# Three products of a weight block, to one PSUM bank in a row or to two banks in turn

## The chip, the cores and the metric

The kernel runs on one core of one Trainium2 chip. The time is the device time of one launch in microseconds (us), as the median of several runs. TensorE (PE in the profile) multiplies, with its weight loads in a row of their own (PEld); VectorE (DVE) and ScalarE (ACT) do the elementwise work, and DMAs bring the weights in.

## The reference, cut to what matters

Two transformer-like blocks are applied to one sequence of 512 tokens with 1024 features: a gated linear attention with a convolution branch, pooling, cross-attention to a memory of 256 tokens, two gated feed-forward layers, then a second linear attention, a sliding-window attention and two squared-ReLU layers. Nearly all the arithmetic is products with weight matrices in float32:

```python
h = x @ w_in                                                    # projections, 1024 rows of weights
y = (jax.nn.silu(x @ w_gate) * (x @ w_up)) @ w_down             # ffn, width 2816, twice
u = jax.nn.relu(h @ w_up); y = (u * u) @ w_down                 # mlp, width 4096, twice
```

## The kernel before, in words

**The product.** A float32 product is made from three products of a faster format: each weight tile and each activation tile is split into a high part and a rest (`w_hi`, `w_lo`; `xh`, `xl`), and `mm3` (L629) adds high times high, high times rest and rest times high into one PSUM bank: weights `a[0]` with moving `b[0]`, `a[0]` with `b[1]`, `a[1]` with `b[0]`.

**The units.** Weights come as 207 units of 128x2048 elements (L46), one after the other through two buffers. For each unit SP loads `w_raw`, ScalarE makes `w_hi` (`split_hi`, L1138), VectorE makes `w_lo` (`split_lo`, L1626), and TensorE uses it. ScalarE may overwrite `w_hi` once TensorE has counted the unit as used (`unit_used`).

**Where the change acts.** `feature_unit` (L648) and the first half of a feed-forward chunk, `up` (L890), take a unit as eight blocks (k) of two column halves (m). Half m is summed over k in its own bank. Before, each k issues the three products of m = 0 and then the three of m = 1, so the banks change after every third product. The last product of half 0 raises that bank's `bank_full`, the last product of half 1 raises `unit_used`, which also tells that its bank is full (`full`, L635). `down` (L906), `token_unit` (L663), the stages pool and glr, and all products that aren't of weights keep `mm3` or single products as they are.

**What sets the order.** Each engine runs one program in a fixed order and waits on semaphores. The banks are dealt out ahead (`plan_banks`, L120): successive units of a projection alternate between banks 0, 1 and 2, 3; in the two mlp stages every `up` uses banks 0 and 1, and `down` goes through banks 4 to 7 twice. A unit's readers wait for bank 0's or 2's fullness first and the other's after it: `drain_pair` (ScalarE, L1145), `residual` and `add` (VectorE, L1657, L1675), `mh<-bank,rstd` (L1766), the queries of the window attention (L2221). TensorE waits with `wait_free` for both banks of a unit before its first product.

**The loops.** A feed-forward stage starts with the `up` of chunk 0 ("first"). Then a loop does the `up` of the next chunk ahead of the `down` of the one before. Between stages stand the normalisations: TensorE sums over features with a matrix of ones, ScalarE and VectorE work out mean and root, and VectorE and ScalarE rewrite the activations before TensorE may go on.

Of the kernel before, what the change touches and what calls it, by code (L numbers as in the profile page):

```python
# [29 lines left out]
D, T, P = 1024, 512, 128  # L30
KT = D // P
# [269 lines left out]
def at(i, per, c):  # L301

    return c if i is None else i * per + c
# [71 lines left out]
def build(nc, x, mem, params, consts, table, w_gk2, sinks, w, out):  # L375
    scratch = nc.dram_tensor("rel_scratch", [16, 384], F32, kind="Internal").ap()
    with ExitStack() as ctx:
# [135 lines left out]
        def bank(key):  # L513
            return banks[FILL[key][0]]

        def wait_full(eng, key, i=None):

            b, _, _, unit, n, per = FILL[key]
            if unit is None:
                eng.wait_ge(bank_full[b], at(i, per, n))  # L520
            else:
                eng.wait_ge(unit_used, at(i, per, unit + 1))

        def wait_free(eng, key, i=None):

            b, n, per = FILL[key][:3]
            if n:
                eng.wait_ge(bank_free[b], at(i, per, n))
# [94 lines left out]
        def _(pe):  # L623
            seen = Seen(pe, sem)

            def mm(dst, a, b, start, stop):
                return pe.matmul(dst, a, b, start=start, stop=stop)  # L627

            def mm3(dst, a, b, start, stop):  # L629

                mm(dst, a[0], b[0], start, False)
                mm(dst, a[0], b[1], False, False)
                return mm(dst, a[1], b[0], False, stop)

            def full(ins, key):  # L635
                b, _, _, unit, _, _ = FILL[key]
                ins.then_inc(bank_full[b] if unit is None else unit_used, 1)

            def weights(c, lo, n):
                return w_hi[:, c % 2, lo:lo + n], w_lo[:, c % 2, lo:lo + n]  # L640
# [4 lines left out]
            def xtile(k):  # L645
                return xh[:, k, :], xl[:, k, :]

            def feature_unit(stage, j, src=xtile, n=T, ready=None):  # L648

                c = UNITS[stage] + j  # L650
                if c:
                    pe.wait_ge(w_lo_ready, c + 1)
                for m in range(2):
                    wait_free(pe, (stage, j, m))
                for k in range(KT):
                    if ready:
                        ready(k)
                    for m in range(2):
                        last = mm3(bank((stage, j, m))[:, 0:n], weights(c, k * 256 + m * P, P), src(k), k == 0, k == KT - 1)
                        if k == KT - 1:  # L660
                            full(last, (stage, j, m))

            def token_unit(stage, j, src, tiles, n=256):  # L663

                c = UNITS[stage] + j
                pe.wait_ge(w_lo_ready, c + 1)
                per = 1 if n == P else 2
                each = tiles // per
                for m in range(per):
                    wait_free(pe, (stage, j, m))  # L670
                    for t in range(m * each, (m + 1) * each):
                        o = (t - m * each) * n
                        for k in range(KT):
                            h, l = src(k)
                            last = mm3(bank((stage, j, m))[:, o:o + n], (h[:, t * P:(t + 1) * P], l[:, t * P:(t + 1) * P]),
                                       weights(c, k * n, n), k == 0, k == KT - 1)
                    full(last, (stage, j, m))

            def layer_norm_sums(name, x_at, wait_tile, tiles=KT, all_tiles=False):


                mean_, sq_ = (name, "mean"), (name, "sq")
                if all_tiles:
                    wait_free(pe, mean_)
                    for k in range(tiles - SUMMED):
                        wait_tile(k)
                        mm(bank(mean_)[:, :], ones[:, :], x_at(k), k == 0, False)
                seen.next("sq_used", tiles - SUMMED - 1)
                if not all_tiles:
                    wait_free(pe, mean_)  # L690
                    mm(bank(mean_)[:, :], ones[:, :], sum_x[:, :], True, False)
                wait_free(pe, sq_)
                mm(bank(sq_)[:, :], ones[:, :], sum_q[:, :], True, False)
                for k in range(tiles - SUMMED, tiles):
                    wait_tile(k)
                    last = mm(bank(mean_)[:, :], ones[:, :], x_at(k), False, k == tiles - 1)
                full(last, mean_)
                squares_of_last(sq_, tiles)
# [33 lines left out]
            def filler(stage):  # L732

                for j in range(2):
                    if stage[:2] == "mk":
                        feature_unit(stage, j, mem_src, MEM)
                    else:
                        token_unit(stage, j, mem_src, MT)

            def linear_attention(name, chunk, q, k, states, kend, kpad, v_at, dv, filler):  # L740
# [5 lines left out]
                def unit(j):  # L746
                    if filler:
                        stage, jj = filler[j]
                        if stage == "mk0":
                            feature_unit(stage, jj, mem_src, MEM)  # L750
                        else:
                            token_unit(stage, jj, mem_src, MT)
# [130 lines left out]
            def chunks(name, ready):  # L883


                U, base, gate = UNITS[name], chunk_base[name], gated[name]
                hh, hl = (fhh, fhl) if gate else (mhh, mhl)
                k_ = 2 if gate else 1

                def up(tag, c, i=None, ready=None):  # L890
                    for which in ("g", "u") if gate else ("u",):
                        pe.wait_ge(w_lo_ready, at(i, per, c + 1))
                        for m in range(2):
                            wait_free(pe, (name, tag, which, m), i)
                        for k in range(KT):
                            if ready:
                                ready(k)
                            for m in range(2):
                                last = mm3(bank((name, tag, which, m))[:, :], weights(c, k * 256 + m * P, P), xtile(k),
                                           k == 0, k == KT - 1)  # L900
                                if k == KT - 1:
                                    full(last, (name, tag, which, m))
                        ready = None
                        c += 1

                def down(tag, c, chunk, i=None):  # L906
                    pe.wait_ge(w_lo_ready, at(i, per, c + 1))
                    pe.wait_ge(sem["h_ready"], at(i, 4, 2 * (base + chunk) + 2))
                    for m in range(KT):
                        key = (name, tag, "d", m)  # L910
                        wait_free(pe, key, i)
                        for k in range(2):
                            last = mm3(bank(key)[:, :], weights(c, k * D + m * P, P),
                                       (hh[:, chunk % 2, k, :], hl[:, chunk % 2, k, :]), k == 0, k == 1)
                        full(last, key)

                per = 2 * (k_ + 1)
                trips = LOOP_TRIPS[gate]
                up("first", U, ready=ready)
                c = U + k_  # L920
                with pe.Fori(0, trips) as i:
                    up(0, c, i)
                    down(0, c + k_, 0, i)
                    up(1, c + k_ + 1, i)
                    down(1, c + 2 * k_ + 1, 1, i)
                c += trips * per
                if not gate:
                    up("late", c)
                    down("late", c + k_, 2 * trips)
                    c += k_ + 1  # L930
                down("last", c, 2 * trips + (0 if gate else 1))
# [18 lines left out]
            for key, src in ((("memn", "mean"), mk[:, :, :]), (("memn", "sq"), mv[:, :].rearrange("p (k t) -> p k t", k=KT))):  # L950
                wait_free(pe, key)
                for k in range(KT):
                    last = mm(bank(key)[:, 0:MEM], ones[:, :], src[:, k, :], k == 0, k == KT - 1)
# [24 lines left out]
            for l in range(2):  # L978
# [10 lines left out]
                if l == 0:  # L989
                    filler(FILLER["ffnn0"])  # L990

                    c = UNITS["pool"]
                    pe.wait_ge(w_lo_ready, c + 1)
                    for m in range(KT):
# [4 lines left out]
                        for k in range(2):  # L999
                            last = mm3(bank(("pool", 0, m))[:, :], weights(c, (2 * g + k) * 256 + (m % 2) * P, P),  # L1000
                                       xtile(2 * g + k), k == 0, k == 1)
# [4 lines left out]
            c = UNITS["glr"]  # L1006
            pe.wait_ge(w_lo_ready, c + 1)
            wait_free(pe, ("glr", 0, 0))
            for k in range(KT):
                tile_ready(k)  # L1010
                last = mm3(bank(("glr", 0, 0))[:, :], weights(c, k * P, P), xtile(k), k == 0, k == KT - 1)
# [1359 lines left out]
```

## Time and profile before

| | |
|---|---|
| median of 3 runs | 2668.21 us (2667.69 to 2670.3) |
| profiled execution, span from first to last instruction | 2667.9 us |
| PE busy | 2525.6 us (95%), 11776 matmuls |
| PEld busy | 2048.8 us (77%) |
| DVE busy | 1507.3 us (56%) |
| ACT busy | 881.7 us (33%) |
| DMA, mean | 85 GB/s |

The only time of the profiled execution itself that the profile gives is its span, 2667.9 us; it stands 0.3 us under the median of the runs. A busy PE counts pipelined matmuls whose ends are modelled, so the distance from one start to the next tells the rate, and not the duration. The 40 digits of a slice line are the span in equal parts, tenths busy.

### The profile page before, as it was taken

To read this page: it belongs to the slowest core of one execution; us is meant where nothing else is said; L and a number is where in the kernel's file an instruction comes from. 1 tells how busy PE (TensorE), PEld (TensorE's weight loads), DVE (VectorE), ACT (ScalarE), POOL (GpSimd) and SP (SyncE) were. 2 spreads that over 40 slices of the span, in tenths; PEclk is the share of its full clock that TensorE was granted. 3 is DMA by queue.
4 is the path that set the end of the run, shared out by engine and by line. 5 is a ranking of instruction groups with operands and counts; after the bars stand their busy time and mean duration, and the time that the engine had idled before them with its cause. 6 is when DMAs were issued, how large, how long until landed. Compare 5 with 4: busy or idle time off the path is not lost.

```text
span 2667.9 us, 29702 instructions
## 1 busy us (share of the span) xinstructions
PE 2525.6 (95%) x11776; PEld 2048.8 (77%) x11776; DVE 1507.3 (56%) x2043; ACT 881.7 (33%) x1184; POOL 9.9 (0%) x23
## 2 busy tenths in 40 slices
PE   8998999999999698999998998999999978999998
PEld 7897777788887576888885797788888766788886
DVE  6887534644445835544447436566665566566666
ACT  3434443422223633322225234322222445322222
POOL 0000000000000000000000000000000000000000
PEclk9999999999999899999998999999999988999999
DMA  5222221222222111222221220232222200222221
GB/s 182 79 80 79 79 79 64 95 95 94 96 96 91 64 63 64 92 97 95 94 94 53 95 95 17 98 110 94 94 94 95 79 32 23 89 95 94 94 94 63
DMA packets 32815, 225.56 MB, mean 85 GB/s; under 512 B 3765, under 2 KB 3813, under 8 KB 6368
## 3 DMA queue, kind: packets, MB, share of 16 engines
q1 hardware_dynamic: 31536, 220.21, 24.0%
q0 software_dynamic: 1200, 4.23, 0.4%
q8 instruction: 57, 0.93, 0.1%
q14 instruction: 22, 0.18, 0.0%
HBM read 222.30 MB, written 2.12 MB: 84 GB/s over the span
## 4 chain that ended last, share of the span: by engine, by line
PE 83%; DVE 10%; ACT 5%; issue 1%; DMA 0%; DVEq 0%; SPq 0%; ACTq 0%
PE bank L627 83%; DVE w_lo L1626 2%; ACT w_hi L1138 1%; ACT xh L1151 1%; ACT xs L1197 1%; DVE cacc L1814 1%; DVE xs L1709 1%; DVE xl L1634 0%; DVE mh L2239 0%; DVE rmax L2258 0%; DVE xs L1723 0%; DVE gs L1865 0%; ACT mh L1589 0%; DVE mh L2255 0%; DVE xs L1678 0%
## 5 line engine op out<-in xcount | busy, mean ns | idle before, releaser
L627 PE MATMUL bank<-xh,w_hi 128*128 128x512 f32 x2040 | 816.5, 400 | 66.1 <-DVE xl L1634 29.4
L627 PE MATMUL bank<-xl,w_hi 128*128 128x512 f32 x2040 | 805.9, 395 | 0.0
L627 PE MATMUL bank<-xh,w_lo 128*128 128x512 f32 x2040 | 804.4, 394 | 0.0
L1626 DVE TENSOR_TENSOR w_lo<-w_raw,w_hi 128x2048 fp32r<-128x2048 f32 x205 | 469.6, 2291 | 411.8 <-ACT w_hi L1138 411.2
L1138 ACT ACTIVATE w_hi<-w_raw 128x2048 fp32r<-128x2048 f32 x205 | 391.4, 1909 | 415.6 <-PE bank L627 415.4
L627 PEld LDWEIGHTS bank<-xh,w_hi 128*128 128x128 f32 x2040 | 389.7, 191 | 170.4 <-DVE xl L1634 31.3
L627 PEld LDWEIGHTS bank<-xh,w_lo 128*128 128x128 f32 x2040 | 389.7, 191 | 83.4
L627 PEld LDWEIGHTS bank<-xl,w_hi 128*128 128x128 f32 x2040 | 390.4, 191 | 82.2 <-issue 2.2
L1678 DVE TENSOR_TENSOR xs<-xs,bank 128x512 f32<-128x512 f32 x448 | 295.4, 685 | 133.4 <-PE bank L627 127.6
L627 PE MATMUL bank<-mhh,w_lo 128*128 128x512 f32 x512 | 204.1, 399 | 0.0
L627 PE MATMUL bank<-mhl,w_hi 128*128 128x512 f32 x512 | 202.0, 395 | 0.0
L627 PE MATMUL bank<-mhh,w_hi 128*128 128x512 f32 x512 | 201.1, 393 | 0.0
L1766 DVE TENSOR_TENSOR mh<-bank,rstd 128x512 f32<-128x512 f32 x64 | 43.9, 691 | 179.7 <-PE bank L627 179.7
L1260 ACT ACTIVATE mhh<-mh 128x512 fp32r<-128x512 f32 x64 | 39.5, 632 | 318.3 <-DVE mh L1771 318.3
L627 PE MATMUL bank<-fhl,w_hi 128*128 128x512 f32 x352 | 139.6, 396 | 0.0
L627 PE MATMUL bank<-fhh,w_lo 128*128 128x512 f32 x352 | 139.5, 396 | 0.0
L627 PE MATMUL bank<-fhh,w_hi 128*128 128x512 f32 x352 | 139.5, 396 | 0.0
L1157 ACT ACTIVATE sq<-xs 128x512 f32<-128x512 f32 x88 | 54.6, 630 | 193.2 <-DVE xs L1678 71.3
L627 PEld LDWEIGHTS bank<-mhl,w_hi 128*128 128x128 f32 x512 | 96.1, 188 | 24.5
L627 PEld LDWEIGHTS bank<-mhh,w_hi 128*128 128x128 f32 x512 | 96.2, 188 | 23.0
L627 PEld LDWEIGHTS bank<-mhh,w_lo 128*128 128x128 f32 x512 | 96.1, 188 | 22.4
L1764 DVE TENSOR_TENSOR fh<-sil,bank 128x512 f32<-128x512 f32 x44 | 30.0, 688 | 116.5 <-PE bank L627 109.5
(287 smaller groups left out, 2630.6 us busy)
## 6 DMA issues: line engine op xcount, KB each, us to landing
w_raw<-weights_in SPq DMA_DIRECT2D x205, 1024.0 KB, 4.9
xs<-x_in SPq DMA_DIRECT2D x4, 512.0 KB, 8.1
sf<-rel_scratch POOLq DMA_DIRECT2D x1, 2048.0 KB, 12.3
y_out<-xs SPq DMA_DIRECT2D x8, 256.0 KB, 2.2
w_raw<-weights_in SPq DMA_DIRECT2D x2, 512.0 KB, 6.9
mk<-mem_in POOLq DMA_DIRECT2D x1, 1024.0 KB, 8.7
sum_q<-consts_in POOLq DMA_DIRECT2D x1, 256.0 KB, 8.8
scan<-consts_in POOLq DMA_DIRECT2D x1, 256.0 KB, 2.8
```

The costliest lines, as they stand in the source:

```text
L627: return pe.matmul(dst, a, b, start=start, stop=stop)
L1138: act.activation(w_hi[:, c % 2, :], w_raw[:, c % 2, :], ACT.Copy).then_inc(w_hi_ready, 1)
L1151: give(act.activation((xh if dst is None else dst)[:, k, :], src, ACT.Copy, **kw), "x_hi")
L1157: give(act.activation(sq[:, k % 2, :], src, ACT.Square), "sq_ready")
L1197: give(act.activation(xs[:, k, :], xs[:, k, :], ACT.Identity, scale=col(f"{param}_g{l}", k), bias=col(f"{param}_b{l}", k)), "xn_ready")
L1260: give(act.activation(hh[:, chunk % 2, m, :], src, ACT.Copy), "hh_ready")
L1626: dve.tensor_tensor(w_lo[:, c % 2, :], w_raw[:, c % 2, :], w_hi[:, c % 2, :].bitcast(F32), ALU.subtract)\
L1678: free(dve.tensor_tensor(xs[:, k, :], xs[:, k, :], bank(key)[:, :], ALU.add), key)
L1709: centred[k] = steps.step(dve.tensor_tensor(x_at(k), x_at(k), mean[:, :], ALU.subtract))
L1764: free(dve.tensor_tensor(hid[:, m, :], sil[:, m, :], bank(key)[:, :], ALU.mult), key)
L1766: free(dve.tensor_tensor(hid[:, chunk % 2, m, :], bank(key)[:, :], rstd[:, :], ALU.mult), key)
L1814: ins = dve.scalar_tensor_tensor(a, u, wj, a, ALU.mult, ALU.add)
```

## The change

A new helper `mm3_pair` takes both halves of one k and issues each kind of product for half 0 and then for half 1. So the six products of a k are the same ones, each bank still gets its three in the same order, and the bank and the weights change at every product. The number of instructions, the buffers, banks and waits are the same. What raises `bank_full` and `unit_used` is still the last product of each half.

```diff
+            def mm3_pair(dst, a, b, start, stop):
+
+                for m in range(2):
+                    mm(dst[m], a[m][0], b[0], start, False)
+                for m in range(2):
+                    mm(dst[m], a[m][0], b[1], False, False)
+                return [mm(dst[m], a[m][1], b[0], False, stop) for m in range(2)]
+
@@ feature_unit
-                    for m in range(2):
-                        last = mm3(bank((stage, j, m))[:, 0:n], weights(c, k * 256 + m * P, P), src(k), k == 0, k == KT - 1)
-                        if k == KT - 1:
-                            full(last, (stage, j, m))
+                    w0, w1 = weights(c, k * 256, P), weights(c, k * 256 + P, P)
+                    last = mm3_pair((bank((stage, j, 0))[:, 0:n], bank((stage, j, 1))[:, 0:n]), (w0, w1), src(k), k == 0, k == KT - 1)
+                    if k == KT - 1:
+                        for m in range(2):
+                            full(last[m], (stage, j, m))
@@ up (inside chunks)
-                            for m in range(2):
-                                last = mm3(bank((name, tag, which, m))[:, :], weights(c, k * 256 + m * P, P), xtile(k),
-                                           k == 0, k == KT - 1)
-                                if k == KT - 1:
-                                    full(last, (name, tag, which, m))
+                            last = mm3_pair([bank((name, tag, which, m))[:, :] for m in range(2)],
+                                            [weights(c, k * 256 + m * P, P) for m in range(2)], xtile(k), k == 0, k == KT - 1)
+                            if k == KT - 1:
+                                for m in range(2):
+                                    full(last[m], (name, tag, which, m))
```

## Rows read from the trace of the kernel before

**Rows 1.** The page: engines' busy time, and the granted clock in 40 slices.
```profile
PE 2525.6 (95%) x11776; PEld 2048.8 (77%) x11776; DVE 1507.3 (56%) x2043; ACT 881.7 (33%) x1184; POOL 9.9 (0%) x23
...
PEclk9999999999999899999998999999999988999999
```

**Rows 2.** The page: the chain that ended last, by engine.
```profile
PE 83%; DVE 10%; ACT 5%; issue 1%; DMA 0%; DVEq 0%; SPq 0%; ACTq 0%
```

**Rows 3.** Timeline of PE, `up` in mlp0: start us, us, engine, line, tiles.
```profile
1799.85 0.39 PE L627 MATMUL bank<-xh,w_hi 128*128 128x512 f32 x1
1800.08 0.39 PE L627 MATMUL bank<-xl,w_hi 128*128 128x512 f32 x1
1800.30 0.39 PE L627 MATMUL bank<-xh,w_lo 128*128 128x512 f32 x1
1800.53 0.39 PE L627 MATMUL bank<-xh,w_hi 128*128 128x512 f32 x1
...
1808.46 0.39 PE L627 MATMUL bank<-xh,w_lo 128*128 128x512 f32 x1
```

**Rows 4.** Timeline of PE, a unit of mk0, 256 columns.
```profile
165.22 0.28 PE L627 MATMUL bank<-meml,w_hi 128*128 128x256 f32 x1
...
170.74 0.28 PE L627 MATMUL bank<-memh,w_lo 128*128 128x256 f32 x1
```

**Rows 5.** Timeline of PE, the `down` behind the `up`.
```profile
1808.69 0.40 PE L627 MATMUL bank<-mhh,w_hi 128*128 128x512 f32 x1
...
1819.67 0.40 PE L627 MATMUL bank<-mhh,w_lo 128*128 128x512 f32 x1
```

**Rows 6.** Timeline, `first` to the next `up` in mlp0.
```profile
1729.79 1.37 DVE L1766 TENSOR_TENSOR mh<-bank,rstd 128x512 f32<-128x512 f32 x2 [1.30 <-PE bank L627]
...
1731.31 0.47 PE L627 MATMUL bank<-xh,w_hi 128*128 128x512 f32 x1 [0.88 <-DVE mh L1766]
```

**Rows 7.** Timeline of ACT and DVE, third unit of xq0.
```profile
373.78 1.29 ACT L1143 ACTIVATE qf<-bank 128x512 f32<-128x512 f32 x2 [5.59 <-PE bank L627]
374.97 1.90 ACT L1138 ACTIVATE w_hi<-w_raw 128x2048 fp32r<-128x2048 f32 x1
...
376.90 2.29 DVE L1626 TENSOR_TENSOR w_lo<-w_raw,w_hi 128x2048 fp32r<-128x2048 f32 x1 [10.67 <-ACT w_hi L1138]
```

**Rows 8.** Timeline of DVE behind the second unit of q.
```profile
132.73 2.29 DVE L1626 TENSOR_TENSOR w_lo<-w_raw,w_hi 128x2048 fp32r<-128x2048 f32 x1 [0.93 <-ACT w_hi L1138]
```

**Rows 9.** Timeline of DVE and ACT, end of mixo.
```profile
315.73 1.38 DVE L1680 SCALAR_TENSOR_TENSOR xs<-xs,bank 128x512 f32<-128x512 f32 x2 [3.59 <-PE bank L627]
...
320.90 0.58 ACT L1169 ACTIVATE mean<-bank 128x512 f32<-128x512 f32 x1
```

**Rows 10.** Timeline of DVE, last unit of sq.
```profile
2164.32 1.37 DVE L2221 SCALAR_TENSOR_TENSOR sf<-bank,rstd 128x512 f32<-128x512 f32 x2 [9.52 <-PE bank L627]
```

**Rows 11.** Timeline of PE, start of mlp1 behind so.
```profile
2294.47 0.47 PE L627 MATMUL bank<-xh,w_hi 128*128 128x512 f32 x1 [2.41 <-DVE xl L1635]
```

**Rows 12.** Timeline, end of xo0, and start of mlp0 behind go.
```profile
462.46 1.37 DVE L1680 SCALAR_TENSOR_TENSOR xs<-xs,bank 128x512 f32<-128x512 f32 x2 [3.59 <-PE bank L627]
...
464.66 1.88 PE L627 MATMUL bank<-xs,ones 128*128 128x512 f32 x4
...
466.58 0.60 ACT L1169 ACTIVATE mean<-bank 128x512 f32<-128x512 f32 x1 [0.29 <-PE bank L627]
...
1714.98 0.75 DVE L1635 SCALAR_TENSOR_TENSOR xl<-xs,prm,xh 128x512 fp32r<-128x512 f32 x1 [0.79 <-ACT xh L1151]
...
1715.88 0.82 PE L627 MATMUL bank<-kk,tab 33*16 33x384 f32 x2 [2.42 <-DMA kk<-consts_in]
```

**Rows 13.** Timeline of DVE and PEld in a `down` of mlp0.
```profile
1786.08 1.37 DVE L1766 TENSOR_TENSOR mh<-bank,rstd 128x512 f32<-128x512 f32 x2 [6.00 <-PE bank L627]
...
1793.36 2.50 DVE L1678 TENSOR_TENSOR xs<-xs,bank 128x512 f32<-128x512 f32 x4
...
1794.74 0.19 PEld L627 LDWEIGHTS bank<-mhh,w_hi 128*128 128x128 f32 x1
```

## The prediction

> **What bounds the kernel now.** I read the page first. TensorE is busy 95% of the span and its clock is at nine tenths or more in 36 of 40 slices [rows 1]; the next engine, VectorE, has 56%. The chain that ended last goes through TensorE for 83% of the span, through VectorE for 10% and ScalarE for 5% [rows 2]. So two things can move the time: the step from one matmul to the next inside the weight units, and the places between stages where TensorE waits for somebody who reads a unit's banks. Then I read the timeline: first the step in a long stretch without waits, then each hand-off that the change can touch.
>
> **How many matmuls change.** By the list of stages, 126 units go through `feature_unit` or `up` with `xh` and `xl`: 50 of projections and 76 of the four feed-forward stages. With 8 x 2 x 3 = 48 each that is 6048 matmuls of 512 columns, about half of the 11776. The one unit of sk with `yh` (48) and the eight mk units of 256 columns (384) come on top. Nothing is added or removed; only their order changes, and with it (a) who follows whom on TensorE and (b) when each bank is told to be full.
>
> **(a) The step.** In an `up` before, 39 starts lie from 1799.85 to 1808.46, so 38 steps take 8.61 us, 226.6 ns each [rows 3]. Look at the four rows in a row there (a tile pair is written moving first: `xl,w_hi` is high weights with the rest of x): high-high to high-rest 0.23 us, high-rest to rest-high 0.22, rest-high to the next high-high 0.23. The first of these keeps the weights and the bank and changes the moving tile. The second changes weights and moving tile in the same bank. The third always changes the bank; it comes once with the same moving tile (half 0 to half 1) and once with the next k's. All steps agree within the 0.01 us in which the rows are written, and three of them make 0.68 us throughout. If a change of bank cost or saved time, the third would stand out. After the change the six steps of a k are three that change weights and bank under the same moving tile, and three that change weights, bank and moving tile. Both are kinds of which the old third step consists. So I take 226.6 ns for all 6048 and 0 us for the step.
>
> The bounds are wide. From below: a unit of mk0 with 256 columns takes 5.52 us for 46 steps, 120.0 ns [rows 4]. So 256 columns more cost 106.6 ns, 512 columns 213.2, and 13.4 ns of each step don't depend on the columns. If these were some hazard of writing one bank in a row, which ends with the change, 6048 x 13.4 ns = 81 us would go. From above: a `down` in the same stage takes 10.98 us for 47 steps, 233.6 ns [rows 5], so operands can change the step by 7.0 ns; on all 6048 that is 42 us. Neither end is near the rows that have the same operands as the new order, so I stay at 0. The same goes for sk and mk: 432 matmuls x 7.0 ns is 3 us at most, and I take 0.
>
> The Trainium skill has a formula for this step (TensorE: Matmul & The Clock Gate, section "Back-to-back issue gap"): N/2.4 + 2.5 ns at full clock. For 512 columns that is 216 ns, and the trace disagrees: 226.6 ns. Were the difference a matter of the order, the change would bring 6048 x 10.8 ns = 65 us; by the formula as it stands, which names no bank, nothing would change. The measured step decides.
>
> **(b) When a bank is full.** Of a unit's last six products, half 0 ended with the third and now ends with the fifth, two steps or 0.45 us later. Half 1 ends with the sixth as before, so `unit_used`, and all weight traffic that hangs on it, keep their times. Half 0's reader runs first and half 1's right behind it on the same engine. On VectorE both reads together take 1.36 to 1.38 us, 0.69 each, and before, the first ended as the second became possible; now the second queues up, and the pair ends 0.45 us later. On ScalarE a read behind a read starts 0.5 us after it; in the 1.29 us of the pair at 373.78 [rows 7] the second, 0.60 us long, started at 374.47, when its bank was full, and would now start at 373.78 + 0.45 + 0.50 = 374.73: some 0.27 us later.
>
> In the steady part this is hidden: between two units that use the same banks lies another unit or a `down` of over 10 us. What remains are the places where somebody waits for the reader. I went through the waits of TensorE of over 0.4 us and traced each back:
>
> - mlp0 and mlp1, `first` to the next `up`: both use banks 0 and 1. VectorE reads both banks from 1729.79 to 1731.16, and TensorE, idle for 0.88 us, goes on at 1731.31 [rows 6]. The pair of reads starts 0.45 us later: 2 x 0.45 = 0.91 us.
> - xq0 and xq1, third unit: ScalarE reads, then makes `w_hi`, VectorE `w_lo` and then `pr`, for which TensorE waits with the transposes [rows 7]. No gap in that chain: 2 x 0.27 = 0.54 us.
> - q, second unit: ScalarE's reads, four logarithms, `w_hi`, then VectorE, which had been idle 0.93 us for it [rows 8] and is then busy until the linear attention can start: 0.27 us.
> - mixo, last unit: VectorE adds at 315.73; ScalarE's squares, a table load and `w_hi` follow without idle time, and so does the mean at 320.90, which shows no wait of its own [rows 9]: 0.45 us.
> - sq, last unit: VectorE's reads at 2164.32 stand at the head of its window-attention work, after 9.52 us idle [rows 10]: 0.45 us.
> - so, last unit: adds, `xh`, `xl`, and TensorE starts mlp1 at 2294.47 after 2.41 us of waiting for that `xl` [rows 11]: 0.45 us.
>
> The sum is 0.91 + 0.54 + 0.27 + 0.45 + 0.45 + 0.45 = 3.07 us. Each of them lies between nothing (some other wait ends last) and 0.69 us (a full VectorE read): 0 to 5.5 us for the eight.
>
> Three places look alike and cost nothing. At the end of xo0 TensorE is busy with sums over earlier tiles, and takes the late tiles from 464.66 on, where the first add was done at 463.15; ScalarE waited 0.29 us for TensorE's mean before it took it [rows 12], and what is left of the delay there ends in front of the squares' sum, which TensorE delivers later still. xo1 has the same shape. At the start of mlp0 TensorE waits to 1715.88 for a DMA that hangs on `unit_used` [rows 12], and its two small matmuls last to 1716.70; `xl` is there at 1715.73 before and 1716.18 after.
>
> One cover has to hold 32 times. In each `down` of the mlps VectorE runs without a pause from the reads of the `up` at 1786.08 on. Its third `xs` add, the first of the four from 1793.36 and done at 1794.05, frees the bank for the weight load at 1794.74 [rows 13]. That is 0.69 us to spare, of which 0.45 go; 0.24 are left.
>
> Own time of the profiled execution: 2667.9 + 3.1 = 2671.0 us; the median of the runs is 0.3 above it, so 2671.3 us.
>
> **The rivals.**
>
> 1. The readers are hidden everywhere, because at each of the six kinds of place another wait ends last. For it: the chain changes engines hundreds of times and passes near ties, and where the clock is at half, a shift by 0.4 us can swap one tie for another. Against: the rows above show chains without idle time. 2668.2 us.
> 2. Slower by the step. The new order brings two neighbourhoods that the old one lacks: while `xl` streams, a `w_hi` block is loaded, and while `xh` streams, a `w_lo` block (before, `w_lo` was loaded only beside `xl`). If such a pair reads in each other's way as the operands of a `down` do, two of six steps cost 7.0 ns more: 2016 x 7.0 = 14 us, in all 2685 us. It decides from 1 ns per new pair on, since 2016 ns with the 3 us of (b) are at the limit of what can be told. Against: the steps of an `up` are equal whether `w_hi` or `w_lo` is loaded beside them [rows 3].
> 3. Slower by the bank cover in `down`. If the delay that reaches the third add is not 0.45 but above 0.69 us, TensorE stops in each of 32 `down`s; at 0.2 us each that is 6.4 us, in all 2678 us.
> 4. Faster: part of the 13.4 ns goes. Half of it would be 6048 x 6.7 = 41 us, 2630 us. Against: the change of bank was already there at every third step and did not show.
> 5. The change doesn't do what it says: were TensorE to reorder its matmuls, neither (a) nor (b) would appear, and the time would be rival 1's. The trace shows them in program order, so I count it there.
>
> **How the numbers follow.** Forecast (b alone) 0.62, own range 2669 to 2674; rival 1 0.14, rival 2 0.11, rival 3 0.07, rival 4 0.06. What this kernel's measurement can tell from no change is about 0.2%, 5.3 us, so 2662.9 to 2673.5 is "same". Faster is rival 4: 0.06. Slower is rivals 2 and 3 and the top of the forecast's own range (0.04): 0.22. Same: 0.72. The range, 2666 to 2680, holds the forecast, rival 1, rival 3 and the small end of rival 2, and leaves out rival 4 and most of rival 2.
>
> **What would show it right or wrong.** In the timeline of an `up` the order `xh,w_hi` twice, `xl,w_hi` twice, `xh,w_lo` twice, still 0.68 us for three. Before the second `up` of mlp0 TensorE waits about 0.45 us longer than now, 1.3 instead of 0.88. VectorE's pair at the third xq unit unchanged in length, but `w_hi` 0.27 us later behind it. In `down` the third add ends some 0.24 us ahead of its weight load. The prediction is wrong if the mean step in `up` differs from 226.6 ns by 1 ns or more (6 us), or if rows of TensorE in the mlp `down`s show waits.

## The result

The changed kernel takes 2672.84 us (median of 19 runs, 2669.6 to 2681.71); the kernel before took 2667.98 us beside it (19 runs, 2665.02 to 2671.51). The ratio is 1.0018, with a 95% interval of 1.0011 to 1.0025. Forecast were 2671.3 us and "within 0.2%". The time is within the range, and the ratio just within the 0.2%; but its interval lies wholly above 1, so the change does cost something. Together with the runs beside the first experiment, 30 runs of the changed kernel have a mean of 2672.6 us and 54 of the one before 2668.8: 3.9 us more, give or take 1.3. The two sessions differ by more than that: 5.4 us more, give or take 1.6, in the first and 2.1, give or take 1.4, in the second.

The profiled execution took 2674.04 us, its span 2672.3 (before: 2667.9; 2671.0 had been forecast). From the page of the changed kernel, the lines that answer to [rows 1] and [rows 2]:

```profile
PE 2528.7 (95%) x11776; PEld 2050.4 (77%) x11776; DVE 1496.2 (56%) x2043; ACT 875.9 (33%) x1184; POOL 9.9 (0%) x23
...
PEclk9999999999999799999998999999999998999999
...
PE 83%; DVE 10%; ACT 5%; issue 1%; DMA 0%; DVEq 0%; SPq 0%; ACTq 0%
```

VectorE and ScalarE are busy 11 and 6 us less for the same work. The timeline shows why: their reads of two banks now stand in one piece. So the pairs are read faster, but they start later. Lines of the helpers are 9 higher than before from here on (L1626 is L1635).

**The step.** Timeline of PE in an `up` of mlp0 and the `down` behind it (start us, us, engine, line, tiles; x2 is two matmuls in one row), which answers to [rows 3] and [rows 5], and under it two rows of a unit of mk0, for [rows 4]:

```profile
1804.17 0.62 PE L627 MATMUL bank<-xh,w_hi 128*128 128x512 f32 x2
1804.62 0.61 PE L627 MATMUL bank<-xl,w_hi 128*128 128x512 f32 x2
1805.08 0.62 PE L627 MATMUL bank<-xh,w_lo 128*128 128x512 f32 x2
...
1810.52 0.62 PE L627 MATMUL bank<-xh,w_lo 128*128 128x512 f32 x2
1810.97 0.40 PE L627 MATMUL bank<-mhh,w_hi 128*128 128x512 f32 x1
...
1822.18 0.63 PE L627 MATMUL bank<-xh,w_hi 128*128 128x512 f32 x2
```

```profile
165.08 0.40 PE L627 MATMUL bank<-meml,w_hi 128*128 128x256 f32 x2
...
170.36 0.41 PE L627 MATMUL bank<-memh,w_lo 128*128 128x256 f32 x2
```

The order is the new one. From 1804.17 to 1810.97 there are 30 steps in 6.80 us, 226.7 ns each, as before; the `down` has 48 in 11.21 us, 233.5 ns; mk0 44 in 5.28 us, 120.0 ns. Over all steps with `xh` and `xl` at full clock (those of up to 300 ns) the mean is 227.28 ns before and 227.25 after. The two kinds of neighbours that only the new order has, `xl,w_hi` behind `xl,w_hi` and `xh,w_lo` behind `xh,w_lo`, have 227.2 and 227.3 ns.

**The hand-offs.** First, timeline from `first` to the next `up` in mlp0 (in brackets the idle time before, and what ended it), for [rows 6]:

```profile
1732.14 1.29 DVE L1775 TENSOR_TENSOR mh<-bank,rstd 128x512 f32<-128x512 f32 x2 [1.75 <-PE bank L627]
...
1733.57 0.70 PE L627 MATMUL bank<-xh,w_hi 128*128 128x512 f32 x2 [1.25 <-DVE mh L1775]
```

TensorE's wait grew from 0.88 to 1.25 us, by 0.37 and not by 0.45. The reason stands in the row above it: VectorE's pair takes 1.29 us where it took 1.37. Then the rows that answer to [rows 7] (third unit of xq0), [rows 8] (behind the second unit of q), [rows 9] (end of mixo), [rows 10] (last unit of sq) and [rows 11] (start of mlp1), all from the timeline of the changed kernel:

```profile
372.46 1.09 ACT L1152 ACTIVATE qf<-bank 128x512 f32<-128x512 f32 x2 [5.79 <-PE bank L627]
373.43 1.91 ACT L1147 ACTIVATE w_hi<-w_raw 128x2048 fp32r<-128x2048 f32 x1
375.37 2.29 DVE L1635 TENSOR_TENSOR w_lo<-w_raw,w_hi 128x2048 fp32r<-128x2048 f32 x1 [10.67 <-ACT w_hi L1147]
```

```profile
132.49 2.29 DVE L1635 TENSOR_TENSOR w_lo<-w_raw,w_hi 128x2048 fp32r<-128x2048 f32 x1 [0.92 <-ACT w_hi L1147]
```

```profile
314.04 1.28 DVE L1689 SCALAR_TENSOR_TENSOR xs<-xs,bank 128x512 f32<-128x512 f32 x2 [3.59 <-PE bank L627]
...
319.11 0.58 ACT L1178 ACTIVATE mean<-bank 128x512 f32<-128x512 f32 x1
```

```profile
2168.03 1.29 DVE L2230 SCALAR_TENSOR_TENSOR sf<-bank,rstd 128x512 f32<-128x512 f32 x2 [9.40 <-PE bank L627]
...
2298.72 1.19 PE L627 MATMUL bank<-xh,w_hi 128*128 128x512 f32 x2 [2.79 <-DVE xl L1644]
```

ScalarE's pair went from 1.29 to 1.09 us, so it ends 0.45 - 0.20 = 0.25 us later; the wait for `xl` at mlp1 went from 2.41 to 2.79.

For [rows 10] the delay behind the pair can be read too. From the last product of sq to the first transpose (`ident,mh`) of the window attention, timeline of PE before and then after; in the row of two the last product is the second, at 2167.83:

```profile
2164.57 0.39 PE L627 MATMUL bank<-xh,w_lo 128*128 128x512 f32 x1
...
2166.82 1.41 PE L1113 MATMUL bank<-ident,mh 128*128 128x128 f32 x8
```

```profile
2167.61 0.61 PE L627 MATMUL bank<-xh,w_lo 128*128 128x512 f32 x2
...
2170.45 0.66 PE L1122 MATMUL bank<-ident,mh 128*128 128x128 f32 x4
```

It takes 2.26 us before and 2.62 after, 0.36 more, at full clock in both. All six traces that have the new order at the last k of `feature_unit` show 2.62 us, the other eight 2.26 or 2.27.

**The places that were to cost nothing.** Timeline at the end of xo0 and the start of mlp0, for [rows 12], and in a `down`, for [rows 13]:

```profile
461.40 1.28 DVE L1689 SCALAR_TENSOR_TENSOR xs<-xs,bank 128x512 f32<-128x512 f32 x2 [3.59 <-PE bank L627]
...
465.07 0.60 ACT L1178 ACTIVATE mean<-bank 128x512 f32<-128x512 f32 x1
...
1714.30 0.75 DVE L1644 SCALAR_TENSOR_TENSOR xl<-xs,prm,xh 128x512 fp32r<-128x512 f32 x1 [0.79 <-ACT xh L1160]
...
1714.77 1.46 PE L627 MATMUL bank<-kk,tab 33*16 33x384 f32 x2 [2.36 <-DMA kk<-consts_in]
```

```profile
1788.81 1.29 DVE L1775 TENSOR_TENSOR mh<-bank,rstd 128x512 f32<-128x512 f32 x2 [6.45 <-PE bank L627]
...
1796.01 2.48 DVE L1687 TENSOR_TENSOR xs<-xs,bank 128x512 f32<-128x512 f32 x4
...
1797.02 0.19 PEld L627 LDWEIGHTS bank<-mhh,w_hi 128*128 128x128 f32 x1
```

From the add to the mean in xo0 it was 4.12 us and is 3.67, and ScalarE's 0.29 us of waiting are gone: the delay went into that slack. In the `down` the first of the four adds ends at 1796.01 + 0.69 = 1796.70, which leaves 0.32 us to the weight load; 0.24 had been forecast, 0.69 were there. The cover held: mlp0 behind its `first` takes 346.85 us before and 346.86 after, mlp1 343.99 and 343.99.

### The profile page after: what moved, and what is told of

Its sections match the earlier page's. It is cut to its first block, busy times and chain, and to the rows that moved or that the text cites. A ratio compares the mean times of both kernels' runs of the same rounds, so it can differ in the third digit from the quotient of the medians.

```text
span 2672.3 us, 29702 instructions
## 1 busy us (share of the span) xinstructions
PE 2528.7 (95%) x11776; PEld 2050.4 (77%) x11776; DVE 1496.2 (56%) x2043; ACT 875.9 (33%) x1184; POOL 9.9 (0%) x23
## 4 chain that ended last, share of the span: by engine, by line
PE 83%; DVE 10%; ACT 5%; issue 1%; DMA 0%; DVEq 0%; SPq 0%; ACTq 0%
PE bank L627 82%; DVE w_lo L1635 2%; ACT w_hi L1147 1%; ACT xh L1160 1%; ACT xs L1206 1%; DVE cacc L1823 1%; DVE xs L1718 1%; DVE xl L1643 0%; DVE mh L2248 0%; DVE rmax L2267 0%; DVE xs L1732 0%; DVE gs L1874 0%; ACT mh L1598 0%; DVE mh L2264 0%; DVE xs L1687 0%
## 5 line engine op out<-in xcount | busy, mean ns | idle before, releaser
L627 PE MATMUL bank<-xh,w_hi 128*128 128x512 f32 x2040 | 654.8, 402 | 65.5 <-DVE xl L1643 27.3
L1635 DVE TENSOR_TENSOR w_lo<-w_raw,w_hi 128x2048 fp32r<-128x2048 f32 x205 | 469.7, 2291 | 412.0 <-ACT w_hi L1147 411.4
L627 PE MATMUL bank<-xl,w_hi 128*128 128x512 f32 x2040 | 642.9, 396 | 0.0
L627 PE MATMUL bank<-xh,w_lo 128*128 128x512 f32 x2040 | 641.9, 395 | 0.0
```

The costliest lines, as they stand in the source:

```text
L1635: dve.tensor_tensor(w_lo[:, c % 2, :], w_raw[:, c % 2, :], w_hi[:, c % 2, :].bitcast(F32), ALU.subtract)\
```

## The experiments

There are twelve, in the order in which they are told here, each timed beside the kernel before.

**The changed kernel again**, no edit, as a measure of how far its own times wander.

> The changed kernel once more, in the same session as the next three. Theory R (readers): all of the loss is that half 0's bank is told full two steps (0.45 us) later where someone waits for its reader; its places sum to 3.1 us, the time is before + 3 us, up to + 5 us. Theory S (step): each product with another bank costs something, spread over 6048 matmuls; before + 5 us as well, but then with a mean step in `up` of 227.1 ns or more against 226.6. This run alone does not tell them apart; it is the mark for the others.

Measured: 2670.64 us (11 runs), before 2668.99 (35 runs); ratio 1.0008, interval 0.9999 to 1.0016; span 2669.1. These runs give less than half of the first difference. All hand-offs have the same sizes in both traces (1.25 us before the second `up`, 6.49 us before xq0's transposes). What differs is the clock: its records stand at half (1.2 GHz) for 140.6 us in the first trace of the changed kernel and for 133.1 in this one.

**The new order only for the last k** (the old one at the other seven), and **only for the first seven** (the old one at the last):

```diff
+            def mm3_halves(dst, a, b, start, stop):
+                return [mm3(dst[m], a[m], b, start, stop) for m in range(2)]
...
-                    last = mm3_pair(...)
+                    last = (mm3_pair if k == KT - 1 else mm3_halves)(...)    # last k only
+                    last = (mm3_halves if k == KT - 1 else mm3_pair)(...)    # first seven only
```

> Pair order only at the last k of each unit (6 of 48 products), the old order at the other seven. Theory R: bank 0 is full as late as in the changed kernel, so all of its loss stays: same time as the changed kernel, before + 3 to 5 us; gap in front of the second `up` of the mlps 1.4 us as in the changed kernel. Theory S: one eighth of the loss, before + 0.6 us.

> Pair order at the first seven k of each unit, the old order at the last k: bank 0 is full three steps ahead of the unit's end, as before. Theory R: same time as before, within 1.5 us, and a gap of 1.04 us in front of the second `up` of the mlps as before. Theory S: seven eighths of the loss, before + 4.3 us.

Measured: last k only 2672.94 us, ratio 1.0019 (1.0009 to 1.0029); first seven only 2668.9 us, ratio 1.0 (0.999 to 1.001). TensorE's waits in the two traces (engine, line, what it waited for: us in total, times, longest), first the last k only, then the first seven:

```profile
PE bank L891 <- DVE pr L1965: 5.8, 2, 2.9
...
PE bank L627 <- DVE mh L1779: 2.5, 2, 1.2
```

```profile
PE bank L891 <- DVE pr L1965: 5.2, 2, 2.6
...
PE bank L627 <- DVE mh L1779: 1.8, 2, 0.9
```

Seven eighths of the new order cost nothing; the one k at the end of a unit costs all of it, and by the time at which half 0 is told full. That separates theory (b) from anything in the step, and it is the strongest of these runs, since the two halves of the change differ by 4 us in median.

**`first` of the mlps in banks 2 and 3**, so that the next `up` need not wait for its readers, on top of the change:

```diff
-        b = 2 if gated else 0
+        b = 2 if gated or tag == "first" else 0
```

> The changed kernel, with the `first` up of the two mlp stages in banks 2 and 3, so that the next `up` has free banks. Theory R: the gap of 1.41 us in front of it vanishes in both stages, 2.8 us less than the changed kernel, about the time of before. Rival (cover): what TensorE gains there it waits for again at the next wait (w_lo of the following unit, or the root that VectorE needs for its reads), and the time stays that of the changed kernel.

Measured: 2671.25 us (11 runs, one of them at 2700.57), ratio 1.0017 (0.9995 to 1.004). In the trace the wait is gone; TensorE runs through while VectorE reads:

```profile
1734.48 0.62 PE L627 MATMUL bank<-xh,w_lo 128*128 128x512 f32 x2
...
1734.91 1.29 DVE L1775 TENSOR_TENSOR mh<-bank,rstd 128x512 f32<-128x512 f32 x2 [1.75 <-PE bank L627]
1734.94 0.62 PE L627 MATMUL bank<-xh,w_hi 128*128 128x512 f32 x2
```

Both `first` units have the same clock in this trace and in that of the changed kernel, and `first` with the next `up`'s start takes 1.52 us less in mlp0 and 1.49 less in mlp1; the 346.8 and 344.0 us behind them don't change. Yet the span is 2673.5, since the records stand at half clock for 145.9 us. So these 3.0 us can be had back in the trace; the time of the whole kernel is too uneven to show it.

**The new order in `up` alone, and in `feature_unit` alone:**

```diff
-                    last = mm3_pair(...)      # in feature_unit (up alone), in up (feature_unit alone)
+                    last = mm3_halves(...)
```

> The new order in `up` alone; projections and feed-forward units as before. By the theory (no cost of the step, only the hand-off of half 0 at the last block of k): the idle time before the second `up` of mlp0 and mlp1 is 1.41 instead of 1.04 us from start to start beyond one step, 2 x 0.37 = 0.74 us in all, while the transposes of xq0 and xq1 start as in the kernel before (6.24 us); time 0.7 us above before, beside the 3 us that the placing of the half-clock stretches moves. By the rival that the new order in the body costs on each step, `up` has 32 x 48 of its steps and would show more than 227 ns.

> The new order in the units of `feature_unit` alone; `up` as before. By the theory: the mlp gaps are back at 1.04 us, the transposes of xq0 and xq1 start 0.25 us later (6.49), the start of mlp1 0.38 later, mixo's and sq's ends 0.36 later each: 2 x 0.25 + 0.25 + 0.36 + 0.38 + 0.37 = 1.9 us above before. If the effects don't add up (another wait takes their place), unit alone and up alone come out as the full change, 2.6 us, or as nothing.

Measured: `up` alone 2670.43 us, ratio 0.9999 (0.999 to 1.0009); `feature_unit` alone 2671.25 us, ratio 1.0006 (0.9997 to 1.0015); before 2669.53. The times agree with 0.7 and 1.9 us and with zero alike. The waits tell the two apart; first `up` alone, then `feature_unit` alone:

```profile
PE bank L891 <- DVE pr L1965: 5.2, 2, 2.6
...
PE bank L627 <- DVE mh L1779: 2.5, 2, 1.2
```

```profile
PE bank L891 <- DVE pr L1965: 5.7, 2, 2.9
...
PE bank L627 <- DVE mh L1779: 1.8, 2, 0.9
```

Each place reacts to its own part of the change and to nothing else, so the terms add up.

**Half by half**, from the kernel before: units that don't wait for their sources run all 24 products of half 0 and then the 24 of half 1.

```diff
+                    return [(m, k) for m in range(2) for k in range(KT)]
...
-                for k in range(KT):
...
-                    for m in range(2):
+                for m, k in order_of(ready):
```

> The opposite of the change, from the kernel before: in every unit that doesn't wait for its sources one by one, all 24 products of half 0 run first and then the 24 of half 1, so the bank changes once in a unit instead of 15 times, and half 0 is told full 24 steps (5.4 us) before half 1. By the theory a change of bank costs nothing: the step stays 227 ns and the time stays within 1 us of before; a reader of half 0 done earlier gives nothing back, since half 1's comes behind its last product as before. By the rival (a change of bank has a price p either way) the time moves by up to some 14 x 120 x p = 1680 p, 1.7 us per ns.

Measured: 2668.06 us, ratio 0.9994 (0.9985 to 1.0003); step 227.24 ns with `xh` and 227.32 with `xl`. With the changed kernel this makes three densities of bank changes: one in 24 matmuls, one in three, and one in every one, all at 227.2 to 227.3 ns. A change of bank has no price that 5000 steps could show. The traces of first seven only and of half by half say it most sharply: from 1479 us on their low clocks fall at the same times, and through the 2458 matmuls with `xh` and `xl` that are left the starts of the two agree within 0.1 us, although the bank changes at nearly every one of them in the first and once in 24 in most units of the second. Half 0 ready 5.4 us early gave nothing back either.

**Where the operands lie.** The prediction bounded the step by the 7 ns between [rows 3] and [rows 5] without knowing what makes them. Four runs (the eighth to the eleventh) looked for it, all from the kernel before, all by unused memory in front of tiles. The first two were meant to put the rows of the `down` operands on multiples of 64 and of 2048 bytes:

```diff
+        sb(ctx, "pad", [P, 14])               # multiple of 64: behind hdec
...
+        sb(ffn_mem, "pad_ffn", [P, 302])      # multiple of 2048
+        sb(second, "pad_mlp", [P, 318])
```

> The kernel before with 56 bytes of unused memory put in front of the tiles `mem`, `fhh`, `fhl`, `mhh`, `mhl`, `yh`, so that their rows start at a multiple of 64 bytes in each partition, as those of `xh` and `xl` do; they start 8 bytes off it now. It measures what the operand gives to the step: the trace of before has 226.7 ns with `xh` and `xl` and 233.9 ns with `mhh`, `mhl`, `fhh`, `fhl`, `yh`. Theory of the place in memory: the steps of `down` fall to 227 ns, some 2600 x 7 ns = 18 us, time about 2650 us. Rival (what fills these tiles, or the writes beside them, makes the step): 234 ns and 2668 us, no change.

> The kernel before with unused memory in front of the feed-forward and mlp tiles, so that each row of 512 numbers of `fhh`, `fhl`, `mhh`, `mhl` starts at a multiple of 2048 bytes in its partition, as those of `xh` and `xl` do (with a multiple of 64 bytes alone the steps of `down` stayed at 234 ns). Theory of the place, coarser grain: the steps of `down` fall from 234 to 227 ns, some 2600 x 7 ns = 18 us, time about 2650 us. Rival (the region of memory, or what fills these tiles, makes the step): 234 ns, no change.

Measured: 2670.58 us, ratio 1.0004 (0.9995 to 1.0013), and 2667.96 us, ratio 1.0004 (0.9991 to 1.0016). The times didn't move. But the edits didn't do what they say: the size of every tile is rounded up to 32 bytes, and by the addresses in the programs the tiles stood 32 bytes off a multiple of 64 in both, as they do in the kernel before (not 8). These two misses say nothing against a theory of place; the steps of the single products did shift in both (last section). The next run turned it round and moved `xh` and `xl`, which had the good step, by 800 bytes (776 were meant). The tiles behind them moved by 2080 bytes and not by 2048, so they did not keep their offset:

```diff
+        sb(ctx, "pad_a", [P, 194])
         xh = sb(ctx, "xh", [P, KT, T], F32R)
...
         xl = sb(ctx, "xl", [P, KT, T], F32R)
+        sb(ctx, "pad_b", [P, 318])
```

> The kernel before with `xh` and `xl` moved by 776 bytes, so that their rows lie as far off a multiple of 2048 bytes as those of `mhh` do; all later tiles move by 2048 bytes and keep their offset. Theory of the place: the steps with `xh` and `xl` rise from 227 to 234 ns, 6048 x 7 ns = 42 us and as much for the token units, time about 2715 us. Rival: steps unchanged at 227 ns, time within 3 us of before.

Measured: 2700.67 us (4 runs), ratio 1.0121 (1.0105 to 1.0137). Timeline of PE, an `up` of mlp0 and the first row of the `down` behind it:

```profile
1794.36 0.40 PE L629 MATMUL bank<-xh,w_hi 128*128 128x512 f32 x1
...
1805.56 0.39 PE L629 MATMUL bank<-mhh,w_hi 128*128 128x512 f32 x1
```

48 steps in 11.20 us: 233.3 ns, where [rows 3] have 226.6. The step rose as forecast; but the time rose by 31 us, not by 42 or more. Over the whole kernel the mean step with `xh` and `xl` grew by 6.1 ns, which is 37 us for 6048 steps; the token units (256 columns, `xh` as weights) got shorter steps and not longer ones, 118.3 ns for 120.0, about 1 us less in their 575. The rest can be estimated for the two profiled spans, which differ by 29.9 us: the `down` operands, moved along, have shorter steps (`fhh`, `fhl` 233.1 ns for 234.2, `mhh`, `mhl` 233.3 for 233.6), 1.6 us in all, and the clock records stand at half for 130.1 us where they stood for 138.9, worth some 4 us if half of such time is lost. The last of the four put the `down` operands 128 bytes past a multiple of 2048, where `xh`, `xl`, `w_hi` and `w_lo` are:

```diff
+        sb(ffn_mem, "pad_ffn", [P, 280])
+        sb(second, "pad_mlp", [P, 296])
```

> The kernel before with unused memory in front of the feed-forward and mlp tiles, so that `fhh`, `fhl`, `mhh`, `mhl` start in their partition 128 bytes past a multiple of 2048, exactly as `xh`, `xl`, `w_hi` and `w_lo` do. (In the two kernels before that were meant to do it, the tiles ended 32 bytes off a multiple of 64, since each tile's size is rounded up.) Theory of the place: the steps of `down` fall from 234 to 227 ns, 2589 x 7 ns = 18 us, time about 2650 us. Rival (only `xh` and `xl` in their own region of memory get 227 ns): 234 ns, 2668 us.

Measured: 2647.89 us (5 runs, 2646.86 to 2649.77), before 2667.93; ratio 0.9924 (0.991 to 0.9937). Timeline of PE, a `down` of mlp0 and the first row of the `up` behind it:

```profile
1794.69 0.39 PE L629 MATMUL bank<-mhh,w_hi 128*128 128x512 f32 x1
...
1805.57 0.39 PE L629 MATMUL bank<-xh,w_hi 128*128 128x512 f32 x1
```

48 steps in 10.88 us: 226.7 ns, where [rows 5] have 233.6. By stages: mlp0 and mlp1 5.9 us less each, ffn0 and ffn1 4.2 less each, 20.2 in all, and the medians differ by 20.0. It beats both kernels.

**The change with this placing** (the twelfth):

> The changed kernel with the placing of the last run (`fhh`, `fhl`, `mhh`, `mhl` 128 bytes past a multiple of 2048). If the two effects are independent, it is 2.6 us, and with another placing of the half-clock stretches 0 to 5 us, above the last run's 2647.9: about 2650.5. The steps of `down` are then shorter by 0.34 us in a `down` of 48, so the cover of the third add is at stake: if VectorE no longer has the bank free in time (0.24 us were left), TensorE stands in each of the 32 mlp `down`s and the mlp segments, 346.8 and 344.0 us before, fall by less than the 5.4 us that 16 x 48 steps of 7 ns give each.

Measured: 2653.14 us (6 runs, 2648.04 to 2655.94), ratio 0.9945 (0.9931 to 0.9958), against 0.9924 (0.991 to 0.9937) without the change. The two were timed in different sessions. Against the kernel before in its own session, the median is 15.9 us lower with the change and 20.0 us lower without it; the intervals of the two ratios overlap, so a cost of some 4 us is likely by the times, and not shown by them. The two profiled spans are alike (2646.3 against 2646.0). The waits of the change are in the trace (2.5 us for 1.7 in front of the second `up`s, 5.7 for 5.2 in front of the transposes of xq0 and xq1), and the clock made up for them: the stretch of hg and mixo that took 155.3 us in the one took 152.1 in the other. The cover in `down` held with the shorter steps too: mlp0 takes 341.0 us in both.

## Why the forecast was right, and where its sizes were off

**(a) The step: right.** 0 us were forecast, 227.28 and 227.25 ns measured. Rival 2, new neighbourhoods of weights and moving tile, is refuted by the equal steps, and so is rival 4: neither the 13.4 ns nor any part of them hangs on the bank. The Trainium skill's formula in "Back-to-back issue gap" (TensorE: Matmul & The Clock Gate), 216 ns for 512 columns, is met by no order and no placing tried; 226.4 ns is the least mean that a kind of product has in any trace. That section calls the formula the gap of an isolated matmul, which the prediction left out, and gives about 131 ns for a stream of weight loads and matmuls; this case's stream is far from that too.

**(b) The hand-offs: right in place, too large in size on VectorE.** All eight places showed the delay and the three alike ones none. The mis-sized term is the 0.45 us of each VectorE place. I let the pair of reads keep its length when the second queues up. But with both banks full the second read starts 0.60 us behind the first instead of 0.68, so the pair shrinks from 1.37 to 1.29 and its end moves by 0.37:

```
place                        forecast   measured
first -> up, mlp0 and mlp1   2 x 0.45   2 x 0.37   wait 0.88 -> 1.25
xq0, xq1 third unit          2 x 0.27   2 x 0.25   6.24 -> 6.49 to the transposes
q second unit                    0.27       0.25   32.41 -> 32.66 from v to the attention
mixo last unit                   0.45       0.36   17.95 -> 18.31 to xq's first matmul
sq last unit                     0.45       0.36   2.26 -> 2.62 from the last product to the transposes
so last unit                     0.45       0.38   wait 2.41 -> 2.79
sum                              3.07       2.59
```

On ScalarE the prediction did let the second read overlap the first, and its 0.27 was 0.25. One of its signs doesn't fit its own working: it expects "VectorE's pair at the third xq unit unchanged in length", but the reads there are ScalarE's, and by 0.45 and 0.27 us their pair had to get 0.18 us shorter; it got 0.20 shorter.

**Rival 1** (hidden everywhere) falls with the waits of 1.25 and 2.79 us and with the two half experiments. **Rival 3** (the cover in `down`) falls: 0.32 us were left, since the delay that reached the third add was 0.37 and not 0.45. **Rival 5** falls with the order in the timeline.

**What the forecast left out: the clock.** The span grew by 4.4 us, 2.6 of which are the hand-offs. The other 1.8 are a net of gains and losses where the granted clock falls in other places (at half for 140.6 us after and 138.9 before). Followed through the traces 120 matmuls at a time, the distance between the two moves by more than 0.4 us only where their clock records differ or a hand-off lies. The largest single one, by the windows of the trace from the start of mlp0 to the second `up` (busy us and count of PE, PEld, DVE, ACT, POOL, then granted clock, DMA share, GB/s), before and after:

```profile
1713.00:1731.00 18.00, 15.01 (x59) 10.22 (x57) 11.32 (x15) 9.23 (x13) 2.80 (x4) 1.00 0.18 62
```

```profile
1713.00:1733.50 20.50, 17.55 (x56) 11.96 (x56) 10.79 (x15) 9.15 (x13) 2.50 (x4) 0.83 0.22 68
```

Before, TensorE came out of its 2.42 us of waiting for `kk` at 2.4 GHz. After, it had waited 2.36 us, and for 5.1 of the 17.4 us of `first` its records stand at 1.2 GHz: 2.4 us for a wait that was no longer, and 0.6 more for the two small products ahead of it. In six of the fourteen traces the granted clock falls in this `first`: in five of the six that have the new order at the last k of `feature_unit`, and in the one with `xh` and `xl` moved, which has the old order. The sixth with the new order there, the last run, keeps full clock. What decides I can't say from these runs; that it is where the stage falls against the clock's own course is a guess. The same scatter is in the kernel before, whose 35 runs beside the first experiments go from 2664.55 to 2680.29. So 2.6 us is what the change costs where it can be followed, 3.9 give or take 1.3 is what it costs in the mean of the runs, with 2.6 at its lower end; whether the rest is chance or a place where the clock now falls more often stays open.

## What to carry to other kernels

In this kernel, where each product has a weight load of its own, interleaving products over two accumulators costs nothing on TensorE and gains nothing, but it delays the first one's end: keep the old order at least for the last block of the sum, where a reader waits. Two reads that queue on one engine are shorter together than two that wait one by one, so shift a pair's end by the difference (0.37) and not by the delay of the first (0.45). And where two stretches of the same matmuls have different steps, compare where their operands start modulo 256 bytes before looking for a reason in the order.

## What was not expected of the hardware

The step of a 512-column matmul depends on where the moving operand starts in its partition. Over the kernels, by the start modulo 256 bytes, mean step at full clock, with `w_hi` and `w_lo` at 128 throughout:

```
start mod 256   step, ns                     where
128             227                          xh, xl before; fhh, mhh in the eleventh run
0               233.3, in turn 229 and 238   mhh in the tenth
32              234.2                        fhh before, mhh in the eighth
64              233.1                        fhh in the tenth
96              233.4                        fhh in the eighth
160             233.4                        xh, xl in the tenth
224             231.5, 232.3, 237.1          mhh before and in the ninth, fhh in the ninth
```

(The last column names the runs by their place above.) The three values at 224 are of `mhh,w_hi`, `mhl,w_hi` and `mhh,w_lo`; in the ninth run `fhh` takes over just this pattern from `mhh` as it gets the same remainder. A start at a multiple of 1024 (the 0 row) doesn't help, so it isn't alignment as such. Nor need it be 128 past a multiple of 2048, where all tiles of the first row lie: `yh`, moved along in the eleventh run to 640 past one, went from 233.2 ns to 228.0, though only 26 of its steps can be read; 256 and 512 are not told apart. Whether 128 is good in itself, or because the weights are at 128 too, no run here tells, since `w_hi` and `w_lo` never moved. The Trainium skill says that TensorE reads weights and moving operand through two ports and that loading weights "doesn't steal SBUF read bandwidth from the running matmul" (TensorE: Matmul & The Clock Gate, "Step-by-step: what each phase is for"); these runs neither confirm nor refute it, but they do show that the streams are not free of 7 ns a step, 20 us in this kernel, that the placing decides.
